# Even mixer: the logits of both heads of a pair issued together, every second step

## The reference

```
h = x @ w_in                                    # 512 x 1024 times all projections of the mixer
q_b, k_b, v_b = heads of 64 columns of h        # 8 heads; cum_f = cumsum(log_sigmoid(f_in + b_f))
for each block i of 128 queries:
    lb = q_b . k_b / sqrt(64) + cum_f(query) - cum_f(key)     # per head, 128 x (i+1)*128 are causal
    pb = softmax(where(causal, lb, -inf))
    ob = pb @ v_b
    # the other attention ("a"): index scores, top-128 of the keys, softmax over latent keys
m = concat(oa @ w_uv, ob) @ w_o
```

## Time and profile before

| | us |
|---|---|
| median of 3 runs | 2091.16 |
| lowest run | 2090.34 |
| the profiled execution: device time | 2091.37 |
| the profiled execution: span of its trace | 2089.7 |
| PE busy in that span | 2001.9 (96%) |
| DVE busy | 1234.9 (59%) |
| ACT busy | 876.0 (42%) |
| POOL busy | 367.4 (18%) |

### The profile page before, as it was taken

How to read it: one execution, slowest core, us unless ns; L and a number is a source line. 1 busy time by engine, 2 the same in 40 slices (tenths; PEclk the granted TensorE clock), 3 DMA queues, 4 the chain that set the end, 5 groups by cost and what they waited for, 6 DMA issues and landing times. The chain is left out here.

```text
span 2089.7 us, 27303 instructions
## 1 busy us (share of the span) xinstructions
PE 2001.9 (96%) x9702; PEld 1604.1 (77%) x9702; DVE 1234.9 (59%) x1894; ACT 876.0 (42%) x1357; POOL 367.4 (18%) x412
## 2 busy tenths in 40 slices
PE   8899999999999899999999999899998899999998
PEld 6666666888888678768888886888876778888886
DVE  3767657888677646765655335678776553333333
ACT  4434735444422443354443225666556543222221
POOL 0033501110000101000000001677636610000000
PEclk9999999999999999999999999999999999999999
DMA  5511022666445322223233222111110022333321
GB/s 177 153 52 41 1 71 102 197 191 193 147 157 160 111 81 91 81 71 100 90 100 115 96 82 65 46 35 39 61 61 1 23 79 92 99 95 95 117 97 48
DMA packets 52781, 193.95 MB, mean 93 GB/s; under 512 B 5809, under 2 KB 8529, under 8 KB 52313
## 3 DMA queue, kind: packets, MB, share of 16 engines
q1 hardware_dynamic: 44824, 165.18, 24.8%
q0 software_dynamic: 7344, 27.27, 4.2%
q10 hardware_dynamic: 528, 0.40, 0.1%
HBM read 189.15 MB, written 3.68 MB: 92 GB/s over the span
## 5 line engine op out<-in xcount | busy, mean ns | idle before, releaser
L196 PE MATMUL psum<-xH,w_hi 128*128 128x512 f32 x1800 | 723.0, 402 | 39.0 <-DVE xL L1387 18.6
L196 PE MATMUL psum<-xH,w_lo 128*128 128x512 f32 x1800 | 706.1, 392 | 0.0
L196 PE MATMUL psum<-xL,w_hi 128*128 128x512 f32 x1800 | 706.0, 392 | 0.0
L166 DVE TENSOR_TENSOR w_lo<-w_raw,w_hi 128x1024 fp32r<-128x1024 f32 (+1 forms) x273 | 355.0, 1301 | 323.0 <-ACT w_hi L160 322.7
L160 ACT ACTIVATE w_hi<-w_raw 128x1024 fp32r<-128x1024 f32 (+1 forms) x273 | 303.2, 1111 | 418.3 <-PE psum L196 408.9
L196 PEld LDWEIGHTS psum<-xH,w_hi 128*128 128x128 f32 x1800 | 341.5, 190 | 135.2 <-DVE xL L1387 34.4
L196 PEld LDWEIGHTS psum<-xH,w_lo 128*128 128x128 f32 x1800 | 340.7, 189 | 72.6
L196 PEld LDWEIGHTS psum<-xL,w_hi 128*128 128x128 f32 x1800 | 341.4, 190 | 70.3 <-issue 3.1
L196 PE MATMUL psum<-hidH,w_hi 128*128 128x512 f32 x528 | 206.2, 391 | 0.0
L196 PE MATMUL psum<-hidH,w_lo 128*128 128x512 f32 x528 | 205.4, 389 | 0.0
L196 PE MATMUL psum<-hidL,w_hi 128*128 128x512 f32 x528 | 205.4, 389 | 0.0
(11 more groups left out here) (316 smaller groups left out, 2443.9 us busy)
## 6 DMA issues: line engine op xcount, KB each, us to landing
w_raw<-in_up SPq DMA_DIRECT2D x132, 512.0 KB, 3.5
w_raw<-in_down SPq DMA_DIRECT2D x48, 704.0 KB, 4.0
mod_raw<-in_mod POOLq DMA_DIRECT2D x48, 512.0 KB, 3.9
w_raw<-in_sb_in SPq DMA_DIRECT2D x26, 512.0 KB, 3.5
w_raw<-in_ev_in SPq DMA_DIRECT2D x23, 512.0 KB, 3.8
w_raw<-in_od_in SPq DMA_DIRECT2D x20, 512.0 KB, 3.6
w_raw<-in_ev_out SPq DMA_DIRECT2D x8, 512.0 KB, 3.6
w_raw<-in_od_out SPq DMA_DIRECT2D x8, 512.0 KB, 3.6
```

What stands on the lines that cost most here:

```text
L166: nc.vector.tensor_tensor(w_lo[:, s % SPLIT, 0:w.cols], raw[:, s, 0:w.cols], w_hi[:, s % SPLIT, 0:w.cols].bitcast(F32), ALU.subtract).then ...
L196: mm = nc.tensor.matmul(acc, a[:, slot % SPLIT, cut], b[:, k0 + k, :], start=start and n == 0, stop=stop and n == 2)
```

## The change

Every second step issues both heads' logits one after the other; the other steps issue none. The wait in front of the pair is for DVE's read of both units of the pair before, since both banks are written anew; it stands once per pair. Unit 32, the first of kind "a", is issued where it was. Nothing else moves.

```diff
@@ -829,8 +829,8 @@
                     kind, i, h = units[u]
                     n = (i + 1) * P
                     if kind == "b":
-                        if u >= 2:
-                            pe.wait_ge(a["ttr"], u - 1)
+                        if u >= 2 and u % 2 == 0:
+                            pe.wait_ge(a["ttr"], u)
                         tile_there(head_queries(h))
                         tile_there(head_keys(h))
                         l, r = hT[rows(h), head_queries(h), blk(i)], hT[rows(h), head_keys(h), 0:n]
@@ -896,7 +896,10 @@
 
                 def step(s):
                     i, k = (s - UNITS) // HEADS, (s - UNITS) % HEADS
-                    if s <= UNITS:
+                    if s < UNITS and s % 2 == 0:
+                        logits(s)
+                        logits(s + 1)
+                    if s == UNITS:
                         logits(s)
                     if UNITS <= s < len(units) - 1:
                         logits(s + 1)
```

## The result

The changed kernel takes 2079.85 us (median of 5 runs, 2076.68 to 2081.31) against 2091.56 for the kernel before (5 runs: four from 2090.34 to 2092.41, and one of 3371.16 that the comparison of fast runs leaves out). The medians are 11.7 us apart, 0.6%; the recorded ratio is 0.9937, interval 0.9927 to 0.9947, that is 11 to 15 us: well clear of no change, though far within 2%. The forecast was 2078.3, its range 2075.5 to 2084.5. The profiled execution took 2076.68 us, 14.7 less than the one before; 12.7 of them arise up to unit 32, 1.9 behind unit 63, where nothing was changed.

The account below looks back on a forecast made before the run. TensorE was taken to set the pace from first logits to filler; 12.2 us from 15 pairs plus 0.65 at steps 30 and 31 gave 12.85 off 2091.37, 2078.5 profiled and 2078.3 median, range 2075.5 to 2084.5.

Parts of the forecast that it names:

- What bounds the kernel: From first logits to filler, TensorE sets the pace, busy 100.70 of 100.93 us; what it saves comes off the end.
- The fixed part and the empty odd steps: Half the logits groups vanish, odd steps go from L196 straight into transposes at 0.23; each pair saves 0.30 us.
- the sum: Fixed parts plus one unit's passes per pair: 12.2 us for 15 pairs, plus 0.65 at steps 30 and 31, 12.85.
- The overlap: In each logits pair the odd head runs beside the even one, saving one unit's passes, 0.21 to 0.85 us by width.
- the bounds: Limits for the overlap's saving per pair: nothing, or one unit's whole passes, 0.21 to 0.85 us; the second was taken.
- strict program order: Rival from the skill's rule: a logits pair takes three pass times, total saving 8.5 us, 2082.7 us; chance 0.05.
- The sum to step 29: Four groups of four widths, 13.3 us, without the last pair's 1.15: 12.2 us saved in 15 pairs.
- Steps 30 and 31: Around the last pair, filler and L886 unmoved, ScalarE's exponential and second emptying earlier, unit 32 gains 0.65 us, at most 0.92.
- The new wait: TensorE waits before each pair for DVE's read of the pair before; taken as 0, upper bound 4 us.
- the slack: DVE's margin at the wait before each pair: 1.0 us for 512 keys, 0.7 for 128 keys.
- The slack of 0.2 for ScalarE's copy: Odd step's earlier transposes after a part of six matmuls: at soonest 3.2 after pair start, copy ends at 2.97.
- the stretch to the filler: Sign in the changed profile: from the first logits to L943, the filler, 88 to 89 us.

Follow-up runs that it names:

- The loaded kernels: One unused MAX8 on VectorE added per step of the stretch: changed kernel 2089.46 us, ratio 0.9985; kernel before 2093.03 us, ratio 1.0005.

## Why the prediction was right

- *What bounds the kernel* was right: what TensorE saved between 106.9 and unit 32 (12.7 us) is what the time fell by, within the scatter of the runs (11.7 between the medians).
- *The fixed part and the empty odd steps*: transposes 0.23 after L196, as taken from the earlier trace rows. With both units on one half, so without any overlap, 5.3 us to unit 30 remained; the sum had 15 x 0.30 = 4.5. An odd step with transposes saves some 0.05 more than the sum's terms: with 512 keys it went from 1.68 to 0.47 us between its L196 matmuls, 1.21, where the sum has 0.30 + 0.85 = 1.15. In 14 odd steps that is 0.7.
- *The overlap*: 1.06 for a pair of 512 keys, forecast 1.05. Putting both on one half costs 7.7 us: 6.9 up to unit 30 and 0.8 in step 30. By the sum's terms the 15 pairs are 2 x 4 x 1.067 - 0.85 = 7.7; 0.7 of them is missing because the changed kernel's two waits for ScalarE are gone there. That both figures read 7.7 is chance. The choice between the bounds by the earlier trace rows was the whole forecast, and it held. The Trainium skill's rule ("TensorE: Matmul & The Clock Gate", Part 3) of strict program order would have made it 1.48, if each head's two passes are issued one behind the other. So taken the trace disagrees with it, as it did before the change. In what order the passes are issued no run shows, and with the heads' passes alternating (two at 145.5, two at 146.0) the order would hold.
- *The sum to step 29*: unit 30 starts 85.0 us after the first logits, where it was 97.2: 12.2, as summed. But two errors cancel in it, which is luck: the 0.7 that the odd steps save beyond the sum, and about as much that the two waits for ScalarE took (a step of 0.76 us where its likes have 0.37, one of 2.15 where they have 1.81).
- *Steps 30 and 31*: 8.07 from the pair to unit 32, forecast 8.0; 0.58 gained, not 0.65. The chain was the forecast's: the exponential no longer stands between the two emptyings. But by it the gain from the filler to unit 32 is only 0.39 (6.59 to 6.20), since the first emptying lasts 0.60, as the earlier trace rows shows, and was counted as 0.5, and the second starts 1.19 after L886, not 1.06. The pair takes 0.08 of that back (1.13 to the transposes, not 1.05), and the wait that is gone in step 30 adds 0.27: a term mis-sized by a quarter of a microsecond and one missed.
- *The new wait*: 0.2 us, taken as 0. The loaded kernels show that the slack was sized well (0.74 a pair). The slack of 0.2 for ScalarE's copy was worked out for one kind of step only; the two waits came in others. The Trainium skill ("TensorEngine Tiling (Array Packing)", PSUM Bottleneck) warns that faster matmuls may leave the emptying of PSUM as the bound; this case's trace comes near that point (VectorE, with all its work, is busy for 86%) but not over it.
- *Wrong*: the stretch to the filler was announced as 88 to 89 us and is 86.9. The step was a slip: I took the 100.93 of the earlier trace rows, which runs to 207.83, inside the filler, for its start at 206.16. And the 1.5 us between forecast and median is not in this stretch. It lies in what the rest does from run to run: in the traces, the time after unit 63's second matmul starts was 1824.4 to 1829.7 us.

## What to carry to other kernels

Two matmuls that contract over 64 partitions each, on different halves, cost as much as one when they are issued back to back into different banks, the only way tried here: look for them in different steps, where a full-width product parts them. Before merging, look for a group of the same form in the trace, the best price there is, best of all one of unequal widths. And compare the queues that fed the later unit: a merge that costs nothing can leave the next edit little room, as the extra VectorE work and the transposes moved ahead showed.

## What the runs showed that I had not expected

The granted clock fell to its lower level right at unit 32 in four profiles, for some 7 to 10 us (a mean of 0.62 over 9.0 us, at levels of 1.0 and 0.5, is 6.8; 0.60 over 12.3 is 9.8), and cost 3.1 to 4.6 us each time, a quarter to over a third of what the change gains. TensorE had done the same before it in profiles where the clock stayed at 1.00: filler, two groups of latent queries, waits of 0.2 and 0.8 us. What makes it fall stays open. And a switch between whole array, half rows and half columns has a price of its own, 0.15 us here, that can be had back by order alone once its operands are early enough.
